# Splitting a weight tile ahead of an activation in the plain networks, and alternating products with outputs in a recurrent mixer

## The reference

```python
def rms_norm(x, g, eps=NORM_EPS):
    x32 = x.astype(jnp.float32)
    y = x32 * lax.rsqrt(jnp.mean(x32 * x32, axis=-1, keepdims=True) + eps)
    return (y * g.astype(jnp.float32)).astype(x.dtype)

def swiglu(h, w_gate, w_up, w_down):
    return (jax.nn.silu(h @ w_gate) * (h @ w_up)) @ w_down

x = x + 0.5 * swiglu(rms_norm(x, ffn_norm[layer, 0]), ...)   # networks 0 and 2
...                                                          # the mixer
x = x + 0.5 * swiglu(rms_norm(x, ffn_norm[layer, 1]), ...)   # networks 1 and 3

def rwkv7_step(state, inp):                                  # the recurrent mixer's step
    r_t, w_t, k_t, v_t, a_t, b_t = inp
    sa = jnp.einsum('bhvk,bhk->bhv', state, a_t)
    state = (state * w_t[:, :, None, :] + sa[..., None] * b_t[:, :, None, :]
             + v_t[..., None] * k_t[:, :, None, :])
    return state, jnp.einsum('bhvk,bhk->bhv', state, r_t)
```

## Time and profile before

| what | value |
|---|---|
| median of 3 runs | 2751.03 us (2749.18 to 2754.38) |
| the profiled execution's own time | 2748.28 us |
| its span, first to last instruction | 2746.4 us |
| granted TensorE clock, mean | 0.997 |
| PE busy | 2689.8 us (98%) |
| DVE busy | 2116.2 us (77%) |
| ACT busy | 1291.1 us (47%) |
| POOL busy | 109.6 us (4%) |
| HBM read | 453.09 MB, 165 GB/s over the span |

### The profile page before, as it was taken

How to read it: one execution, slowest core, us unless ns; L and a number is a source line. 1 busy time by engine, 2 the same in 40 slices (tenths; PEclk the granted TensorE clock), 3 DMA queues, 4 the chain that set the end, 5 groups by cost and what they waited for, 6 DMA issues and landing times.

```text
span 2746.4 us, 51122 instructions
## 1 busy us (share of the span) xinstructions
PE 2689.8 (98%) x20542; PEld 2492.2 (91%) x20542; DVE 2116.2 (77%) x3203; ACT 1291.1 (47%) x1781; POOL 109.6 (4%) x109
## 2 busy tenths in 40 slices
PE   8999999999999999999999999999999999999999
PEld 8998799999888989999969999986899989859998
DVE  7985589899755648984977877599777777987777
ACT  5345553443532315344565444546554464464543
POOL 0000000000013310000000000000000000000000
PEclk9999999999999999999999999999999999999999
DMA  6754267667331016764414554431344544304444
GB/s 268 277 228 154 92 257 273 236 253 279 142 138 62 1 71 230 275 229 169 154 62 154 184 181 173 165 140 47 110 168 183 183 154 144 148 16 154 156 183 152
DMA packets 61231, 456.21 MB, mean 166 GB/s; under 512 B 6841, under 2 KB 6865, under 8 KB 8737
## 3 DMA queue, kind: packets, MB, share of 16 engines
q1 hardware_dynamic: 54432, 395.83, 39.2%
q0 software_dynamic: 6656, 58.35, 5.3%
HBM read 453.09 MB, written 1.07 MB: 165 GB/s over the span
## 4 chain that ended last, share of the span: by engine, by line
PE 84%; DVE 8%; ACT 3%; DMA 3%; issue 1%; DVEq 0%; SPq 0%; ACTq 0%
PE ps L760 18%; PE ps L601 14%; PE ps L602 14%; PE ps L603 14%; PE ps L1041 3%; DMA ring<-in_weights 3%; PE ps L1438 3%; DVE half_parts L2324 1%; PE ps L1445 1%; ACT arena L2049 1%; PE ps L1297 1%; PE ps L1131 1%; PE ps L1124 1%; PE ps L544 1%; DVE w_parts L2120 1%
## 5 line engine op out<-in xcount | busy, mean ns | idle before, releaser
L1585 ACT ACTIVATE w_parts<-ring 128x1024 fp32r<-128x1024 f32 x462 | 462.9, 1051 | 410.2 <-PE ps L601 310.8
L2120 DVE SCALAR_TENSOR_TENSOR w_parts<-ring,w_parts 128x1024 fp32r<-128x1024 f32 x462 | 544.3, 1219 | 54.8 <-ACT w_parts L1585 54.6
L760 PE MATMUL ps<-stream_high,half_parts 128*128 128x256 f32 x2224 | 427.0, 288 | 2.1 <-DVE half_parts L2324 2.1
L2324 DVE SCALAR_TENSOR_TENSOR half_parts<-ring,half_parts 128x1024 fp32r<-128x1024 f32 x225 | 271.8, 1213 | 145.3 <-ACT half_parts L1672 144.7
L760 PEld LDWEIGHTS ps<-stream_high,half_parts 128*128 128x128 f32 x2224 | 351.9, 190 | 7.5 <-issue 6.7
L601 PE MATMUL ps<-act_parts,w_parts 128*128 128x256 f32 x1232 | 347.0, 282 | 5.6 <-DVE act_parts L2120 4.0
L601 PE MATMUL ps<-h_parts,w_parts 128*128 128x256 f32 x1200 | 341.5, 285 | 8.4 <-DVE w_parts L2120 8.4
L602 PE MATMUL ps<-act_parts,w_parts 128*128 128x256 f32 x1232 | 348.1, 283 | 0.0
L603 PE MATMUL ps<-act_parts,w_parts 128*128 128x256 f32 x1232 | 347.9, 282 | 0.0
L602 PE MATMUL ps<-h_parts,w_parts 128*128 128x256 f32 x1200 | 340.3, 284 | 0.0
L603 PE MATMUL ps<-h_parts,w_parts 128*128 128x256 f32 x1200 | 340.1, 283 | 0.0
(11 more groups left out here) (456 smaller groups left out, 5182.3 us busy)
## 6 DMA issues: line engine op xcount, KB each, us to landing
ring<-in_weights SPq DMA_DIRECT2D x374, 1024.0 KB, 4.8
arena<-in_mod_weights POOLq DMA_DIRECT2D x32, 1536.0 KB, 8.2
arena<-in_cond POOLq DMA_DIRECT2D x8, 512.0 KB, 6.3
arena<-toeplitz_rows POOLq DMA_DIRECT2D x1, 1536.0 KB, 12.2
x<-in_x SPq DMA_DIRECT2D x1, 1024.0 KB, 4.8
arena<-in_ctx POOLq DMA_DIRECT2D x1, 1024.0 KB, 5.6
out<-x SPq DMA_DIRECT2D x1, 1024.0 KB, 3.9
const<-in_const SPq DMA_DIRECT2D x1, 975.0 KB, 11.3
```

Source lines behind the costliest of these rows:

```text
L760: mm = pe.matmul(into, stationary, moving, start=start and n == 0, stop=stop and n == 2, skip_group_check=True)
L1585: a(w_parts[:, to, 0, cols], ring[:, at, cols], ACT.Copy).then_inc(s["w_high"], 1)
L2120: return stt(out=out, in0=whole, scalar=1.0, in1=high, op0=ALU.mult, op1=ALU.subtract)
L2324: stt(out=half_parts[:, u % 3, 1, :], in0=ring[:, (t["tile"] + tile) % RING, half * HALF:(half + 1) * HALF], scalar=1.0, in1=half_parts[:, ...
```

## The change

It has four parts.

1. TensorE sums the network's squares between the two halves of tile 1, not after tile 1 (plain networks).
2. ACT splits tile 3 (`high(3)`) ahead of `scaled_silu(0)`, not behind it. DVE does `low(3)` between `scale_gate(0)` and `scaled_activation(0)`, and `low(4)` ahead of `scale_gate(1)`.
3. In the recurrent mixer TensorE does `products(1, 2)` between the two outputs of chunk 0. ACT copies an output, `strict(6)`, the other output, and the last five bias instructions stand together ahead of `strict(7)`.
4. For this, the masked matrices of groups 2 and 3 of chunk 1 get places of their own, in a tensor that held an operand of the bonus term, and DVE waits for `bonus_done` before it writes there.

```diff
-        early = [spare[:, 2, 512 * b:512 * b + 512].rearrange("p (n t) -> p n t", n=4) for b in range(4)]
-        Arb = [[...], early[0:2] + [carve(26624 + 512 * b, 4, P) for b in range(2, NB)]]
-        Ark = [[...], early[2:4] + [carve(28672 + 512 * b, 4, P) for b in range(2, NB)]]
+        early = [spare[:, 2 - b // 4, 512 * (b % 4):512 * (b % 4) + 512].rearrange("p (n t) -> p n t", n=4) for b in range(8)]
+        Arb = [[...], early[0:2] + early[4:6]]
+        Ark = [[...], early[2:4] + early[6:8]]
@@ TensorE
-                def project(t, i, bank, of):
+                def project(t, i, bank, of, between=None):
                     for m in range(2):
+                        if m and between is not None:
+                            between()
                         arrived(t, i, m)
...
-                    project(1, 0, 1, h_parts).then_inc(s["up_ready"], 1)
-                    if n == 0:
-                        pe.wait_ge(s["const_loaded"], 16)
-                    else:
-                        pe.wait_ge(s["x_ready"], (0, 2, 3, 5)[n] * QUARTERS)
-                    added_norm(n + 1, 3, norm_sq)
+                    def own_norm():
...
+                        added_norm(n + 1, 3, norm_sq)
+
+                    project(1, 0, 1, h_parts, between=own_norm).then_inc(s["up_ready"], 1)
...
                 outputs(0, 0)
+                products(1, 2)
                 outputs(0, 1)
-                products(1, 2)
                 products(1, 3)
@@ ACT
+                high(3)
                 scaled_silu(0)
-                high(3)
                 high(4)
...
-                    if m % 3 == 2:
-                        strict(5 + m // 3)
                     if m == 2:
                         for g in range(2):
+                            strict(5 + g)
                             actv.wait_ge(s["rw_y"], g + 1)
@@ DVE
                 scale_gate(0)
+                low(3)
                 scaled_activation(0)
-                low(3)
...
+                low(4)
                 scale_gate(1)
-                low(4)
                 normed_low()
...
                 masks(5)
+                dve.wait_ge(s["bonus_done"], 1)
                 masks(6)
```

More of the change, by code:

```diff
@@ L324, in build @@
         Aak = [carve(24576 + 512 * b, 4, P) for b in range(NB)]
-        early = [spare[:, 2, 512 * b:512 * b + 512].rearrange("p (n t) -> p n t", n=4) for b in range(4)]
-        Arb = [[carve(26624 + 512 * b, 4, P) for b in range(NB)], early[0:2] + [carve(26624 + 512 * b, 4, P) for b in range(2, NB)]]
-        Ark = [[carve(28672 + 512 * b, 4, P) for b in range(NB)], early[2:4] + [carve(28672 + 512 * b, 4, P) for b in range(2, NB)]]
+        early = [spare[:, 2 - b // 4, 512 * (b % 4):512 * (b % 4) + 512].rearrange("p (n t) -> p n t", n=4) for b in range(8)]
+        Arb = [[carve(26624 + 512 * b, 4, P) for b in range(NB)], early[0:2] + early[4:6]]
+        Ark = [[carve(28672 + 512 * b, 4, P) for b in range(NB)], early[2:4] + early[6:8]]
         Am = [spare[:, 0, 512 * b:512 * b + 512].rearrange("p (n t) -> p n t", n=4) for b in range(NB)]
@@ L711, in ffn @@
                     plain_gate().then_inc(s["gate_ready"], 1)
-                    project(1, 0, 1, h_parts).then_inc(s["up_ready"], 1)
-                    if n == 0:
-                        pe.wait_ge(s["const_loaded"], 16)
-                    else:
-                        pe.wait_ge(s["x_ready"], (0, 2, 3, 5)[n] * QUARTERS)
-                    added_norm(n + 1, 3, norm_sq)
+                    def own_norm():
+                        if n == 0:
+                            pe.wait_ge(s["const_loaded"], 16)
+                        else:
+                            pe.wait_ge(s["x_ready"], (0, 2, 3, 5)[n] * QUARTERS)
+                        added_norm(n + 1, 3, norm_sq)
+                    project(1, 0, 1, h_parts, between=own_norm).then_inc(s["up_ready"], 1)
                     if ahead is not None:
```

## The result

| | before | changed |
|---|---|---|
| median of the runs | 2750.27 us (5 runs) | 2764.03 us (5 runs, 2760.23 to 2766.80) |
| profiled execution, span | 2746.4 us | 2762.0 us |
| TensorE busy | 2689.8 us | 2696.0 us |
| mean granted clock | 0.997 | 0.995 |

The changed kernel is slower: its ratio to the kernel before is 1.0053, with a 95% interval of 1.0042 to 1.0064. Forecast were 2762 us and a change of +11.4 us; measured were 2764.0 and +13.8 between the medians.

The account below looks back on a forecast made before the run. TensorE, busy 98%, was taken to bound the kernel, with tile 3's late transfer setting its stalls. Tile 4 delays +7.96, clock +3.4 and mixer 0 gave +11.4 on 2751.0, forecasting 2762 us, range 2753 to 2768.

Parts of the forecast that it names:

- The transfer bounds tile 3: Plain networks: `high(3)` waits for tile 3's DMA landing, so only 1.0 of 7.2 us of stall can go.
- Tile 4 at the landing + 11.06: Plain networks: tile 4 starts 11.06 us after tile 3's landing, with a 2.84 us TensorE stall in each.
- the 7.96 of the forecast: Four plain networks: tile 4 starts later by 2.56, 0.75, 2.09 and 2.56 us, together 7.96 us.
- Later tiles are hidden: Plain networks: tile 5 is ready at landing + 16.35, wanted at + 16.82, so hidden with 0.47 us to spare.
- The clock behind tile 4: Plain networks: clock falls behind the four new stalls cost 0.85 us each, 3.4 us in all (0 to 6.2).
- The mixer at 0: Recurrent mixer: the new order gains and loses nothing, 0 us, with bounds of -1.2 and +0.5.
- The saved stall comes back in front of step C0: Mixer: the inversion's first step needing all masks still waits for `masks(7)`, at 936.47, so the 1.8 us stall saves 0.
- the upper bound of 0.5: Mixer: at most +0.5 us, from late `masks(5)` and `masks(6)` or clock lost in the longer stall.
- The faster one: Rival, plain networks: engine order decides, stalls before tile 3 and their clock loss go, 8.5 us faster, 2742.5 us; 7%.
- The missing table load: Rival, ACT in plain networks: table load already done during the transfer wait, chain 1.3 us shorter, +2.8, 2754 us; 10%.
- a drain behind the load: Rival, ACT in plain networks: 1.38 us remainder behind each table load, +5.5 us, 2767.5 us; 3%.

Follow-up runs that it names:

- the second trace: The unmodified changed kernel measured and traced once more against the kernel before: ratio 1.0059, medians 2764.4 against 2749.5 us.
- the experiment with silu early: Changed kernel with ACT's order of before (silu of pair 0 ahead of `high(3)`), DVE's new order kept, against the kernel before: ratio 1.0036, +10.7 us.
- part 2 alone: Kernel before with only the ACT and DVE reordering around tiles 3 and 4, against the kernel before: ratio 1.0038, 2759.2 against 2748.5 us.
- the transfer alone: Kernel before with GpSimd's first two 1.5 MB transfers held until tiles 2 and 4 in each plain network, against the kernel before: ratio 0.9995.
- the early sums with the late transfer: Changed kernel with part 2 undone, early sums of squares and the mixer's new order kept, against the kernel before: ratio 0.9998.

## Why the prediction was right, and what it missed

*The transfer bounds tile 3: right.* ACT's `high(3)` is released by the DMA in all four networks (30.79 in network 0), and holding GpSimd's transfers takes that away. The waits before tile 3 are 1.88, 0.66, 1.11 and 1.50 us, 5.2 in sum, where 7.2 - 1.0 = 6.2 was forecast. Most of this microsecond is no gain: with the sum of squares between the halves of tile 1, tiles 1 and 2 take 0.2 us longer in each of networks 1 to 3, 0.7 us in all, so that much of the wait only moved. The rest is network 1's landing, 0.34 us earlier behind the start of tile 1. The landings vary from trace to trace, mostly by a few tenths, in network 3 by more: `high(3)` starts 12.65 us behind tile 1 in the first trace and 11.60 in the second.

*Tile 4 at the landing + 11.06: right.* 41.82 - 30.79 = 11.03, 376.87 - 365.83 = 11.04, in network 3 1084.96 - 1073.92 = 11.04. Link by link it held: silu 3.31 behind the landing (3.34 forecast), DVE 0.67 behind silu. The sum from tile 1 to tile 4 rose by 7.5 us against the 7.96 of the forecast, and by 6.2 in the second trace, where the landing of network 3 was this 1.05 us earlier. The cause is the one given, and the experiment with silu early showed its two shares. The wait's length read 2.6 and not 2.84 us, since the trace counts it from the modelled end of the last matmul; from the start of tile 3 to that of tile 4 it is 8.57 us, 2.81 more than a tile's 5.76.

*Later tiles are hidden: right.* Tile 5 follows tile 4 without a wait.

*The clock behind tile 4: right in size.* The forecast took 0.85 us for each of four stalls, 3.4 in sum. In three traces with this wait of 2.6 us (the changed kernel twice, part 2 alone) the clock fell behind 2, 3 and 2 of the four, and a tile 4 with the fall took 7.3 us instead of 5.8. So there were 7 falls in 12 waits; at 1.5 us each that is 10.5 us in three traces, 3.5 us a run.

*The mixer at 0: the step that failed.* "The saved stall comes back in front of step C0" was right: the distance from `products(1, 1)` to C0 is 14.40 us against 14.32. But the waits that had been apart, 1.77 and 0.67, became 0.51 and 1.85, and behind the 1.85 the clock fell in five of the six traces that have it. It had stayed full in the five traces with the old order. That costs 1.7 us, more than the upper bound of 0.5 that I gave, which had clock in it. I had priced the clock for the longest stalls only, not for one that grew from 0.67 to 1.85.

*Rivals.* The faster one was tried: it needs the landing 2.56 us earlier, and with a landing 5 to 7 us earlier parts 1 and 2 are indeed faster than the kernel before by 7.8 us (8.5 were forecast for it), though only once the two held transfers were kept apart. Without part 2 it is 8.5, so what gains is the early landing with the early norm, not the order of part 2. Where between 0 and 5 us the loss turns into a gain was not tried. The missing table load didn't come about (32.81, behind `high(3)`), nor did a drain behind the load: silu started at 34.10, 0.01 us behind the load's end at 34.09. There the Trainium skill's "What ACT_TABLE_LOAD costs" ("ScalarE: Activation LUTs"), with its drain beside the load, doesn't agree with this trace.

*What stays open.* The networks' 10.5 us and the mixer's 1.7 make 12.2 of the 15.6 us between the first two traces. The rest, 3.4 us, is scattered over stretches that the change doesn't touch. More falls of the clock aren't behind it: outside the stages it fell five times in either trace, though not at the same places (at 298 us, in the attention, in the changed kernel only, at 1933 us in the kernel before only). Between the medians +13.8 and +14.9 were measured, where the two halves measured apart add up to +9.7 (+10.7 for part 2, -1.1 for the changed kernel without it). By the intervals of the ratios this gap is no more than barely clear of chance, and it was not settled.

## What to carry to other kernels

Before an instruction is moved ahead, look at what releases the other one: if it is a transfer, everything that is put behind it loses the time of waiting that it had been hidden in, and here 2.5 us of DVE work and a table load did. When two bounds end close together, trace both and lift them in one step: here the transfer alone brought nothing that could be told (0.9995), the early sums with the late transfer neither (0.9998, with the mixer's new order beside them), and both together 8.5 us. A wait of under 2 us costs more than itself when the clock falls behind it, and two waits made into one can cost what two short ones didn't.

## What the runs showed of the hardware

The clock's fall isn't a matter of a wait's length alone. Behind waits of 1.6 to 1.95 us before tile 3 it came three times in sixteen over the traces of all these kernels (once in four in the kernel before), behind 2.6 us before tile 4 seven times in twelve, and behind 1.85 us at one place in the mixer in five of six. Behind the 1.77 us before `products(1, 3)`, the mixer's wait in the old order, it never came in five. At one and the same wait of one kernel (C0 of the changed kernel) it came in one trace and not in the other.

Tile 3's transfer of 1 MB took 10.3 to 12.2 us from issue to landing beside GpSimd's 4 MB (eight traces), and 4.6 to 6.1 us with two of GpSimd's transfers held (five traces). Holding both until the same point only made another tile late, by 2.9 us of ACT's waiting (the row at 370.49); with them held apart and the sums early, the only wait for a low part left between tiles 1 and 5 was one of 0.5 us in network 3, and none with part 2 too.
